# Latent attention: the value products of a head pair in two blocks in place of five

## The chip, the cores and the metric

The kernel runs on one core of a Trainium2 chip. The metric is the device time of one execution in microseconds; lower is better. Here TensorE is also called PE, VectorE DVE, ScalarE ACT, GpSimd POOL and SyncE SP, as in the profile.

## The reference

Two blocks of a model are computed one after the other on 512 tokens of 1024 channels: feed forward, gated linear attention with a convolution, cross attention and again feed forward; then latent attention, a convolved feed forward, a pooling mixer and a last convolved feed forward. All inputs are float32. The change lies in the latent attention, which sees 16 meta tokens and the 512 tokens, 528 rows. The reference fills these up to 640 and goes through them in tiles of 128 queries:

```python
for start in range(0, L, Q_BLOCK):
    end = start + Q_BLOCK
    qb = q[:, start:end]; kb = k[:, :end]; vb = v[:, :end]
    s = jnp.einsum('bqhd,bkhd->bhqk', qb, kb).astype(jnp.float32) * scale
    s = jnp.where(mask[None, None], s, -jnp.inf)
    p = jax.nn.softmax(s, axis=-1).astype(vb.dtype)
    outs.append(jnp.einsum('bhqk,bkhd->bqhd', p, vb))
o = jnp.concatenate(outs, axis=1).reshape(B, L, N_HEADS * V_HEAD_DIM)
return o @ w_o
```

There are 16 heads, with values of 64 columns each.

## The kernel before

Every engine has its own instruction stream, written out by hand, and waits on semaphores. A `Signal` numbers its events in the order in which one engine produces them (`declare`), so that `wait(engine, key)` is a wait for a count; `pe_mla_order` gives the order of TensorE's events and must agree with the order in which `pe_mla` issues.

The latent attention goes over **8 pairs of heads**. The queries lie in five tiles `j`; tile 0 has the 16 meta rows, tiles 1 to 4 have 128 rows each, and tile `j` sees `j + 1` tiles of keys. A pair takes its tiles in the order `ITEMS = (4, 2, 1, 3, 0)`, each for both heads, which makes **10 turns** a pair and 80 in all (`SEQ`, counter `x`). "Turn 3 of pair 2" is `x = 23`.

What is done for a head and a tile:

- **Scores** (`pe_scores`, L3191): TensorE multiplies queries by keys into PSUM, for tiles 4, 2, 1 as one group and for tiles 3, 0 as the other. The scores of the heads ahead are made at turns 4, 6, 7 and 9 (`SCORES_AT`). A group waits until ScalarE has read the group of the head before it, whose place it takes.
- **Maxima** (L3430, VectorE), **probabilities** (`probs`, L3293, ScalarE: exponent and sum), then the division by the sum (L3440, L3441, VectorE).
- **Turn** (`pe_turn`, L3218): TensorE transposes the probabilities, `j + 1` pieces of 128 x 128, into PSUM pair 2. A tile of four or five pieces and a tile of head one share banks, so a turn waits for ScalarE's copy of the last one or of the one before.
- **Turned copy** (`turned_copy`, L3302): ScalarE copies the turned probabilities to `pt[:, x % 4]`, a ring of four slots with five rows of 128 each; tile `j` uses rows 0 to `j`. It waits for the value products that read the slot before.
- **Value products** (`pe_values`, L3242), one block for a tile and both heads: `j + 1` pieces times 2 heads, values (64 columns) as weights, the copies as moving data. Tile 4 goes to bank 1 of PSUM pair 3, tiles 2, 1, 3, 0 to bank 0. Each f32 product stands as two records in the trace.
- **Halves out** (`upper`, L3308, ScalarE; `lower`, L3446, VectorE): the output, split into `XHI` and `XLO`. Bank 1 is read at turn 5; bank 0 at turn 2 of the next pair. Tile 4's products wait for the read of bank 1 of the pair before, tile 2's for that of bank 0 (`("ol", p - 1, 0)`).

Beside the turns stand **jobs** (`pe_job`, L3171 and L3163): parts of the projections to queries, keys and values of later heads. In even pairs each of the ten turns has a job (`JOB_SLOTS`), in odd pairs turns 0, 1, 4, 6 and 8. Query and value jobs, and half of the key jobs, write bank 1 of PSUM pair 1, so such a job waits until VectorE has read the last one (L3565 for queries). Pair 6 has jobs at turns 0 to 3 alone, pair 7 none; in pair 0, turns 2 and 3 have none.

The place of a value block is set in `pe_mla`: block `y` of the whole sequence stands at turn `x = 2 y + 2`, behind the turn, the scores and the job of it, so at turns 2, 4, 6, 8 of its pair and turn 0 of the next:

```python
for x in range(len(SEQ)):
    pe_turn(pe, x)
    if scores_at(x):
        pe_scores(pe, n, *scores_at(x))
    for job in JOB_AT[x]:
        pe_job(pe, n, job)
    if x % 2 == 0 and x:
        pe_values(pe, n, x // 2 - 1)
```

From turn 1 of pair 7 on, parts of the output projection (L854, L856, L858) go in between, and behind the loop the rest of it.

Of the kernel before, what the change touches and what calls it, by code (L numbers as in the profile page):

```python
# [21 lines left out]
P = 128  # L22
# [3 lines left out]
META = 16  # L26
# [18 lines left out]
MH, NOPE, ROPE, VD = 16, 64, 32, 64  # L45
# [120 lines left out]
def program(nc, ctx, A, out):  # L166
# [2673 lines left out]
    NI = len(ITEMS)  # L2840
# [64 lines left out]
    def scores_at(x):  # L2905
# [5 lines left out]
        return (h, g) if h < MH else None  # L2911

    def pe_mla_order():
        o = [("s", h, g) for h in range(2) for g in range(2)]
        for x in range(len(SEQ)):
            o.append(("t", x))
            if scores_at(x):
                o.append(("s",) + scores_at(x))
            if x % 2 == 0 and x:
                o.append(("pv", x // 2 - 1))  # L2920
        return o + [("pv", len(SEQ) // 2 - 1)]

# [74 lines left out]
    def pe_mla(pe):  # L2997
# [54 lines left out]
# [3 lines that stand above are left out]
                pe_scores(pe, n, *scores_at(x))  # L3055
            for job in JOB_AT[x]:
                pe_job(pe, n, job)
            if x % 2 == 0 and x:
                pe_values(pe, n, x // 2 - 1)
            if x in EARLY_OUT:  # L3060
                pe_mla_out(pe, n + 3 * MH // 4, *EARLY_OUT[x])
        pe_values(pe, n, len(SEQ) // 2 - 1)
        n += 3 * MH // 4
# [157 lines left out]
    def pe_values(pe, n, y):  # L3221
# [14 lines left out]
        act_m.wait(pe, ("tc", 2 * y + 1))  # L3236
        nq = META if j == 0 else P
        for i in range(j + 1):
            for a in range(2):
                h, p0 = 2 * p + a, VD * a  # L3240
                dst = PS[3][p0:p0 + VD, 1, 0:P] if j == 4 else PS[3][p0:p0 + VD, 0, QROW[j]:QROW[j] + nq]
                ins = nc.tensor.matmul(dst, v4[:, h // 4 % 2, i, h % 4 * VD:(h % 4 + 1) * VD], pt[:, (2 * y + a) % 4, i, 0:nq],  # L3242
                                       start=(i == 0), stop=(i == j))
# [20 lines left out]
    def act_mla(act):  # L3264
# [31 lines left out]
        def turned_copy(x):  # L3296
            h, j = SEQ[x]
            pe_m.wait(act, ("t", x))
            if x >= 4:
                pe_m.wait(act, ("pv", x // 2 - 2))  # L3300
            nq = P if j else META
            act_m.inc(nc.scalar.activation(pt[:, x % 4, 0:j + 1, 0:nq], turn_at(x).rearrange("p (i q) -> p i q", q=P)[:, :, 0:nq],  # L3302
                                           ACT.Copy), ("tc", x))
# [1001 lines left out]
```

How the kernel before makes its waits and increments, by code:

```python
    def wait(self, eng, key):  # L124
        eng.wait_ge(self.sem, self.order[key])
# [463 lines left out]
    def slot_free(act, n):  # L589
        if n == MIX_HELD:
            dve_mix.wait(act, ("c", 3))
        elif n == XAT_HELD:
            pe_x.wait(act, ("s", 7))
        elif N_DOWN <= n < N_DOWN + 5:
            act.wait_ge(unit_summed, PHASE["cffn0"] + 4)
        elif N_DOWN + 5 <= n < N_DOWN + 7:
            act.wait_ge(hid_lo, 3 * FT)
        elif N_DOWN + 7 <= n < N_POOL + 4:
            act.wait_ge(unit_summed, N_DOWN)
        elif N_CF1 <= n < N_CF1 + 4:
            act.wait_ge(unit_summed, N_DOWN + 5)
        elif N_CF1 + 4 <= n < N_CF1 + 6:
            act.wait_ge(unit_summed, N_POOL + 4)
        elif n in (LAST + 2, LAST + 3):
            act.wait_ge(unit_summed, LAST)
        elif n >= LAST + 4:
            act.wait_ge(unit_summed, n - 3)
        elif O_OUT + 2 <= n < O_OUT + 5:
            act.wait_ge(unit_summed, O_OUT)
        elif O_OUT + 5 <= n < O_OUT + KD:
            pe_m.wait(act, ("s", MH - 1, 1))
        elif PHASE["cffn0"] <= n < PHASE["cffn0"] + 4:
            pe_m.wait(act, ("pv", len(SEQ) // 2 - 1))
        else:
            act.wait_ge(unit_summed, n - (PHASE["cffn0"] + 4) + O_OUT + 1)
# [31 lines left out]
    def sp_unit(sp, n, it, u):  # L648
# [1 line left out]
        if z and n >= z.n + RAW:  # L650
            v = (n - z.n) // 2 - 2
            sp.wait_ge(st_lo_dve, z.lo_dves + 4 * v + 4)
            if n % 2 == z.n % 2:
                sp.wait_ge(st_lo_pool, z.lo_pools + 3 * v + 2)
            else:
```

## Time and profile before

| | us |
|---|---|
| median of 3 runs | 2193.51 |
| lowest, highest | 2193.27, 2195.99 |
| profiled execution, own time | 2193.65 |
| its span | 2191.9 |
| loop of turns, first turn to last value block | 1170.9 to 1331.4 |
| pairs 2 and 3 together | 1211.29 to 1253.95 |

The profile is of one execution. A timeline row has the start from the span's start and the duration, both in us, the engine, the line of the kernel, the operation, what it writes and reads, its shape and how many records it holds; in brackets stands the idle time ahead of it with what ended it. A matmul's record is about 0.28 us long while the next one may start 0.12 us behind it, so the distance of two starts is what a matmul takes of TensorE's time. The bracket counts idle time from the end of the record before, and is less than what the start is late by.

### The profile page before, as it was taken

What the parts mean: (1) busy time and instruction counts of PE and PEld (TensorE: products, weight loads), DVE (VectorE), ACT (ScalarE), POOL (GpSimd) and SP (SyncE); (2) the same over time, 40 slices, a digit from 0 to 9 for tenths busy, and PEclk for the clock granted to TensorE, in tenths of its full rate; (3) what the DMA queues carried; (4) which work ended last, traced back from release to release, by engine and by line L of the source; (5) the groups of instructions that cost most, each with busy time, mean ns of one, the idle gap of its engine ahead of it and who ended that gap; (6) DMA issues with size and microseconds to landing.
All of it is one profiled execution on the core that took longest, in us unless ns stands there. A gap on an engine that the chain in (4) does not pass through costs nothing.

```text
span 2191.9 us, 37679 instructions
## 1 busy us (share of the span) xinstructions
PE 2163.7 (99%) x14613; PEld 1966.3 (90%) x14613; DVE 1353.5 (62%) x2137; ACT 1004.1 (46%) x1966; POOL 954.3 (44%) x724
## 2 busy tenths in 40 slices
PE   9999999999999999999999999999999999999998
PEld 7899998888888788989998889999999979999897
DVE  6794766637645557839568765762634698536266
ACT  5464553432443435636455556442433565424244
POOL 3644535642482456344452115244444504544443
PEclk9999999999999999999999999999999999999999
DMA  5333333331352223333321113133333303233331
GB/s 171 96 107 104 104 102 95 96 85 45 96 164 68 78 81 112 97 100 112 97 72 33 36 40 107 39 86 97 94 90 89 114 10 101 96 99 94 96 94 70
DMA packets 336811, 195.39 MB, mean 89 GB/s; under 512 B 7469, under 2 KB 327682, under 8 KB 336658
## 3 DMA queue, kind: packets, MB, share of 16 engines
q1 hardware_dynamic: 335570, 191.26, 29.8%
q8 instruction: 101, 1.65, 0.3%
q0 software_dynamic: 432, 0.79, 0.2%
q10 hardware_dynamic: 656, 1.25, 0.2%
q14 instruction: 52, 0.43, 0.1%
HBM read 190.39 MB, written 2.10 MB: 88 GB/s over the span
## 4 chain that ended last, share of the span: by engine, by line
PE 85%; DVE 8%; ACT 3%; issue 2%; POOL 1%; DVEq 0%; DMA 0%; ACTq 0%; SPq 0%; POOLq 0%
PE PS L854 17%; PE PS L858 17%; PE PS L856 17%; PE PS L1288 5%; PE PS L1290 5%; PE PS L1289 5%; PE PS L3191 2%; PE PS L3171 2%; PE PS L1209 2%; PE PS L1211 2%; PE PS L1210 2%; PE PS L3218 1%; PE PS L3242 1%; DVE u_conv L1745 1%; PE PS L2170 1%
## 5 line engine op out<-in xcount | busy, mean ns | idle before, releaser
L774 POOL TENSOR_TENSOR w_lo<-raw,w_hi 128x512 fp32r<-128x512 f32 (+5 forms) x559 | 740.9, 1348 | 920.6 <-ACT w_hi L790 919.0
L790 ACT ACTIVATE w_hi<-raw 128x512 fp32r<-128x512 f32 (+5 forms) x545 | 302.3, 603 | 454.2 <-PE PS L858 351.7
L854 PE MATMUL PS<-XHI,w_hi 128*128 128x264 f32 (+2 forms) x1720 | 412.4, 306 | 0.4 <-POOL w_lo L774 0.3
L858 PE MATMUL PS<-XHI,w_lo 128*128 128x264 f32 (+2 forms) x1720 | 406.2, 302 | 0.0
L856 PE MATMUL PS<-XLO,w_hi 128*128 128x264 f32 (+2 forms) x1720 | 405.7, 302 | 0.0
L854 PEld LDWEIGHTS PS<-XHI,w_hi 128*128 128x128 f32 x1720 | 276.3, 189 | 16.1 <-issue 2.4
L858 PEld LDWEIGHTS PS<-XHI,w_lo 128*128 128x128 f32 x1720 | 276.0, 189 | 12.6
L856 PEld LDWEIGHTS PS<-XLO,w_hi 128*128 128x128 f32 x1720 | 276.0, 189 | 12.1 <-issue 0.7
L854 PE MATMUL PS<-h_hi,w_hi 128*128 128x512 f32 (+2 forms) x588 | 179.7, 341 | 0.7 <-DVE h_lo L1771 0.7
L856 PE MATMUL PS<-h_lo,w_hi 128*128 128x512 f32 (+2 forms) x588 | 179.4, 341 | 0.0
L858 PE MATMUL PS<-h_hi,w_lo 128*128 128x512 f32 (+2 forms) x588 | 179.4, 341 | 0.0
L854 PEld LDWEIGHTS PS<-h_hi,w_hi 128*128 128x128 f32 x588 | 101.6, 188 | 13.8 <-issue 1.3
L858 PEld LDWEIGHTS PS<-h_hi,w_lo 128*128 128x128 f32 x588 | 101.6, 188 | 12.6
L856 PEld LDWEIGHTS PS<-h_lo,w_hi 128*128 128x128 f32 x588 | 101.6, 188 | 12.3
L755 POOL TENSOR_TENSOR w_lo<-raw,w_hi 128x512 fp32r<-128x512 f32 x48 | 67.5, 1409 | 94.9 <-ACT w_hi L1371 94.9
L755 POOL TENSOR_TENSOR sf_lo<-raw,sf_hi 128x512 fp32r<-128x512 f32 x48 | 68.3, 1426 | 78.8 <-ACT sf_hi L1371 78.8
L1533 ACT ACTIVATE h_hi<-hid 128x528 fp32r<-128x528 f32 (+4 forms) x56 | 35.7, 638 | 145.2 <-DVE hid L1769 145.1
L1745 DVE SCALAR_TENSOR_TENSOR u_conv<-u_buf,cols,u_conv 128x528 f32<-128x528 f32 (+1 forms) x44 | 62.3, 1415 | 50.5 <-ACT u_conv L1492 50.5
L1807 DVE SCALAR_TENSOR_TENSOR X<-PS,X 128x512 f32<-128x512 f32 x48 | 33.1, 689 | 86.7 <-PE PS L858 86.7
L1745 DVE SCALAR_TENSOR_TENSOR g_conv<-g_buf,cols,g_conv 128x528 f32<-128x528 f32 (+1 forms) x44 | 54.3, 1235 | 39.1 <-ACT g_conv L1511 39.1
L1771 DVE TENSOR_TENSOR h_lo<-hid,h_hi 128x512 fp32r<-128x512 f32 (+4 forms) x56 | 44.4, 794 | 43.4 <-ACT h_hi L1533 43.4
L1517 ACT ACTIVATE g_act<-g_conv 128x528 f32<-128x528 f32 (+1 forms) x44 | 28.1, 639 | 88.7 <-DVE g_conv L1748 88.7
(621 smaller groups left out, 5472.4 us busy)
## 6 DMA issues: line engine op xcount, KB each, us to landing
raw<-in_ffn_w_up SPq DMA_DIRECT2D x132, 512.0 KB, 3.7
raw<-in_ffn_w_down SPq DMA_DIRECT2D x70, 512.0 KB, 3.8
raw<-in_ffn_w_gate SPq DMA_DIRECT2D x44, 512.0 KB, 3.8
raw<-in_w_in SPq DMA_DIRECT2D x25, 512.0 KB, 3.6
raw<-in_ffn_w_down SPq DMA_DIRECT2D x24, 384.0 KB, 3.4
raw<-in_xattn_w_kv SPq DMA_DIRECT2D x16, 512.0 KB, 3.8
raw<-in_w_out SPq DMA_DIRECT2D x8, 512.0 KB, 4.0
raw<-in_xattn_w_q SPq DMA_DIRECT2D x8, 512.0 KB, 4.6
```

What stands on the lines that cost most here:

```text
L755: ins = nc.gpsimd.tensor_tensor(s_lo, seven_source(z, v, i), s_hi.bitcast(F32), ALU.subtract)
L774: ins = nc.gpsimd.tensor_tensor(d[:, c], r[:, c], h[:, c].bitcast(F32), ALU.subtract)
L790: ins = nc.scalar.activation(d, r, ACT.Copy)
L854: nc.tensor.matmul(ps, wh, ahi(k)[:, c:c + w], start=(k == 0), stop=False)
L856: nc.tensor.matmul(ps, wh, alo(k)[:, c:c + w], start=False, stop=False)
L858: ins = nc.tensor.matmul(ps, wl, ahi(k)[:, c:c + w], start=False, stop=(k == u.kt - 1))
L1209: nc.tensor.matmul(ps, h_hi[:, k, ts], s_hi[:, cs], start=start, stop=False)
L1288: nc.tensor.matmul(bank_, wh, xh, start=(k == 0 and i in (0, 1, 3)), stop=False, skip_group_check=True)
L1289: nc.tensor.matmul(bank_, wh, xl, start=False, stop=False, skip_group_check=True)
L1290: ins = nc.tensor.matmul(bank_, wl, xh, start=False, stop=(k == 3), skip_group_check=True)
L1745: nc.vector.scalar_tensor_tensor(cv_[:, 0:w], buf[:, 1:1 + w], tap(inv - 2, 1, ft), cv_[:, 0:w], ALU.mult, ALU.add).then_inc(conv_mid, 1)
L1771: nc.vector.tensor_tensor(h_lo[:, a + 2 * it, hidden_cols(blk)], hid[:, 0:w], h_hi[:, a + 2 * it, hidden_cols(blk)].bitcast(F32), ALU.subt ...
```

## The change

The value blocks of a pair stand at two turns: the products of tiles 4 and 2 behind the job of turn 3, those of tiles 1, 3 and 0 behind the job of turn 9. Pair 7 keeps its places. `values_at` gives them, for `pe_mla_order` and for `pe_mla`. The turned copy of tile 0 (turns 8 and 9) goes to row 4 of its slot, which only tile 4 uses besides, and no longer waits for the products that read rows 0 to 2 of the slot; the products of tile 0 read row 4. Everything below the new lines stands 7 lines lower in the file.

```diff
--- before.py
+++ after.py
@@ -2910,15 +2910,23 @@
         h = 2 * (x // (2 * NI)) + d
         return (h, g) if h < MH else None
 
+    VALUES_BEHIND = {3: (0, 1), 9: (2, 3, 4)}
+
+    def values_at(x):
+
+        p, at = x // (2 * NI), x % (2 * NI)
+        if p == PAIRS - 1:
+            return ([at // 2 - 1 + NI * p] if at and at % 2 == 0 else []) + ([NI * PAIRS - 1] if at == 2 * NI - 1 else [])
+        return [NI * p + y for y in VALUES_BEHIND.get(at, ())]
+
     def pe_mla_order():
         o = [("s", h, g) for h in range(2) for g in range(2)]
         for x in range(len(SEQ)):
             o.append(("t", x))
             if scores_at(x):
                 o.append(("s",) + scores_at(x))
-            if x % 2 == 0 and x:
-                o.append(("pv", x // 2 - 1))
-        return o + [("pv", len(SEQ) // 2 - 1)]
+            o += [("pv", y) for y in values_at(x)]
+        return o
 
 
     PROBS_AT = {0: ((1, 1),), 1: ((1, 3),), 2: ((1, 0),), 5: ((2, 4),), 6: ((2, 2), (2, 1)), 7: ((2, 3),),
@@ -3055,11 +3063,10 @@
                 pe_scores(pe, n, *scores_at(x))
             for job in JOB_AT[x]:
                 pe_job(pe, n, job)
-            if x % 2 == 0 and x:
-                pe_values(pe, n, x // 2 - 1)
+            for y in values_at(x):
+                pe_values(pe, n, y)
             if x in EARLY_OUT:
                 pe_mla_out(pe, n + 3 * MH // 4, *EARLY_OUT[x])
-        pe_values(pe, n, len(SEQ) // 2 - 1)
         n += 3 * MH // 4
         act_m.wait(pe, ("p", MH - 1, GROUPS[1][-1]))
         pe_out_half(pe, n, 1, 0, ks=range(KD - 1))
@@ -3234,12 +3241,12 @@
         if j == 4 and p % 2 == 0:
             pe.wait_ge(unit_read, n + kv_jobs(p // 2)[0].unit + 1)
         act_m.wait(pe, ("tc", 2 * y + 1))
-        nq = META if j == 0 else P
+        nq, i0 = (META, 4) if j == 0 else (P, 0)
         for i in range(j + 1):
             for a in range(2):
                 h, p0 = 2 * p + a, VD * a
                 dst = PS[3][p0:p0 + VD, 1, 0:P] if j == 4 else PS[3][p0:p0 + VD, 0, QROW[j]:QROW[j] + nq]
-                ins = nc.tensor.matmul(dst, v4[:, h // 4 % 2, i, h % 4 * VD:(h % 4 + 1) * VD], pt[:, (2 * y + a) % 4, i, 0:nq],
+                ins = nc.tensor.matmul(dst, v4[:, h // 4 % 2, i, h % 4 * VD:(h % 4 + 1) * VD], pt[:, (2 * y + a) % 4, i0 + i, 0:nq],
                                        start=(i == 0), stop=(i == j))
         pe_m.inc(ins, ("pv", y))
 
@@ -3296,10 +3303,10 @@
         def turned_copy(x):
             h, j = SEQ[x]
             pe_m.wait(act, ("t", x))
-            if x >= 4:
+            if x >= 4 and j:
                 pe_m.wait(act, ("pv", x // 2 - 2))
-            nq = P if j else META
-            act_m.inc(nc.scalar.activation(pt[:, x % 4, 0:j + 1, 0:nq], turn_at(x).rearrange("p (i q) -> p i q", q=P)[:, :, 0:nq],
+            nq, i0 = (P, 0) if j else (META, 4)
+            act_m.inc(nc.scalar.activation(pt[:, x % 4, i0:i0 + j + 1, 0:nq], turn_at(x).rearrange("p (i q) -> p i q", q=P)[:, :, 0:nq],
                                            ACT.Copy), ("tc", x))
 
         def upper(p, part):
```

TensorE in pair 2, from turn 2 to turn 5, before. `pt,v` are value products, `const,pr` transposes (the turns), `cq,w` a query job, `k,q` scores; the pieces left out are matmuls of the same job or the same scores:

```order
L3218 MATMUL PS<-const,pr 128x128 x3
...
L3171 MATMUL PS<-cq_hi,w_lo 128x264
L3242 MATMUL PS<-pt,v 64x128 x10
L3218 MATMUL PS<-const,pr 128x128 x3
...
L3171 MATMUL PS<-cq_hi,w_lo 128x264
L3218 MATMUL PS<-const,pr 128x128 x2
L3191 MATMUL PS<-k,q 128x512
...
L3171 MATMUL PS<-cq_hi,w_lo 128x264
L3242 MATMUL PS<-pt,v 64x128 x6
L3218 MATMUL PS<-const,pr 128x128 x2
```

And now:

```order
L3178 MATMUL PS<-cq_hi,w_lo 128x264
L3225 MATMUL PS<-const,pr 128x128 x3
L3178 MATMUL PS<-cq_hi,w_hi 128x264
...
L3178 MATMUL PS<-cq_hi,w_lo 128x264
L3249 MATMUL PS<-pt,v 64x128 x16
L3225 MATMUL PS<-const,pr 128x128 x2
L3198 MATMUL PS<-k,q 128x512
...
L3178 MATMUL PS<-cq_hi,w_lo 128x264
L3225 MATMUL PS<-const,pr 128x128 x2
L3178 MATMUL PS<-cq_hi,w_hi 128x264
```

The 10 products of tile 4 stood between the job of turn 2 and turn 3, and the 6 of tile 2 between the job of turn 4 and turn 5. All 16 now stand behind the job of turn 3; jobs 2 and 3, and jobs 4 and 5, have only transposes between them.

TensorE in pair 6, from turn 4 on, where there are no jobs, before:

```order
L3218 MATMUL PS<-const,pr 128x128 x2
L3191 MATMUL PS<-k,q 128x512
L3191 MATMUL PS<-k,q 128x16
L3191 MATMUL PS<-k,q 128x272
L3191 MATMUL PS<-k,q 128x144
L3242 MATMUL PS<-pt,v 64x128 x6
L3218 MATMUL PS<-const,pr 128x128 x6
L3191 MATMUL PS<-k,q 128x400
L3191 MATMUL PS<-k,q 128x16
L3242 MATMUL PS<-pt,v 64x128 x4
L3218 MATMUL PS<-const,pr 128x128 x4
L3191 MATMUL PS<-k,q 128x512
```

And now, from the block of turn 3 on:

```order
L3249 MATMUL PS<-pt,v 64x128 x16
L3225 MATMUL PS<-const,pr 128x128 x2
L3198 MATMUL PS<-k,q 128x512
L3198 MATMUL PS<-k,q 128x16
L3198 MATMUL PS<-k,q 128x272
L3198 MATMUL PS<-k,q 128x144
L3225 MATMUL PS<-const,pr 128x128 x6
L3198 MATMUL PS<-k,q 128x400
L3198 MATMUL PS<-k,q 128x16
L3225 MATMUL PS<-const,pr 128x128 x4
L3198 MATMUL PS<-k,q 128x512
```

Between the two large scores (`128x512`, of heads 14 and 15) stood the products of tiles 2 and 1. Now only transposes and the small scores stand there. On ScalarE and VectorE the instructions and their order are as before; the wait of the two copies of tile 0 in each pair is gone.

## Rows read from the trace of the kernel before

**Rows 1.** The page: the chain that ended last, shares of the span by engine.

```profile
PE 85%; DVE 8%; ACT 3%; issue 2%; POOL 1%; DVEq 0%; DMA 0%; ACTq 0%; SPq 0%; POOLq 0%
```

**Rows 2.** Busy us (x instructions) by stretch: PE, PEld, DVE, ACT, POOL, PEclk, DMA.

```profile
1211.29:1253.95 42.66, 42.30 (x356) 35.62 (x355) 30.04 (x109) 22.55 (x73) 7.73 (x13) 1.00 0.12 33
```

**Rows 3.** Timeline of TensorE, pair 2: start, us, line, out<-in, shape, records [idle before].

```profile
1214.90 0.29 PE L3171 MATMUL PS<-cq_hi,w_lo 128*128 128x264 f32 x1
1215.02 0.49 PE L3218 MATMUL PS<-const,pr 128*128 128x128 f32 x3
1215.71 0.39 PE L3171 MATMUL PS<-cq_hi,w_hi 128*128 128x264 f32 x1 [0.20 <-DVE q L3565]
...
1216.78 0.28 PE L3171 MATMUL PS<-cq_hi,w_lo 128*128 128x264 f32 x1
1216.99 1.31 PE L3242 MATMUL PS<-pt,v 128*64 128x128 f32 x20
1218.24 0.55 PE L3218 MATMUL PS<-const,pr 128*128 128x128 f32 x3
1218.54 0.37 PE L3171 MATMUL PS<-cq_hi,w_hi 128*128 128x264 f32 x1
...
1222.91 0.88 PE L3242 MATMUL PS<-pt,v 128*64 128x128 f32 x12
1223.72 0.44 PE L3218 MATMUL PS<-const,pr 128*128 128x128 f32 x2
...
1225.09 0.60 PE L3218 MATMUL PS<-const,pr 128*128 128x128 f32 x4
1225.52 0.96 PE L3191 MATMUL PS<-k,q 128*128 128x400 f32 x4
...
1228.19 0.66 PE L3218 MATMUL PS<-const,pr 128*128 128x128 f32 x4
1228.69 1.95 PE L3191 MATMUL PS<-k,q 128*128 128x512 f32 x8
```

**Rows 4.** Timeline of TensorE, start of pair 3.

```profile
1236.67 0.29 PE L3242 MATMUL PS<-pt,v 128*64 128x16 f32 x4
1236.91 0.75 PE L3218 MATMUL PS<-const,pr 128*128 128x128 f32 x5
...
1239.00 1.31 PE L3242 MATMUL PS<-pt,v 128*64 128x128 f32 x20
```

**Rows 5.** Timeline of VectorE, pair 2.

```profile
1215.22 0.43 DVE L3565 TENSOR_TENSOR q<-PS,ct 128x264 f32<-128x264 f32 x1 [1.05 <-PE PS L3171]
...
1216.72 0.57 DVE L3446 TENSOR_TENSOR XLO<-PS,XHI 128x400 fp32r<-128x400 f32 x1 [0.53 <-ACT XHI L3308]
1217.21 0.42 DVE L3565 TENSOR_TENSOR q<-PS,ct 128x264 f32<-128x264 f32 x1
...
1223.33 0.43 DVE L3565 TENSOR_TENSOR q<-PS,ct 128x264 f32<-128x264 f32 x1
```

**Rows 6.** Timeline of ScalarE, start of pair 3.

```profile
1236.06 0.71 ACT L3302 ACTIVATE pt<-PS 128x640 f32<-128x640 f32 x1 [1.52 <-PE PS L3218]
```

**Rows 7.** Timeline of VectorE, from turn 7 of pair 2 into pair 3.

```profile
1230.67 0.72 DVE L3430 CUSTOM_DVE_ANT_0 PS<-PS,causal 128x528 f32<-128x528 f32 x1 [1.93 <-PE PS L3191]
...
1240.87 0.57 DVE L3446 TENSOR_TENSOR XLO<-PS,XHI 128x400 fp32r<-128x400 f32 x1
```

**Rows 8.** Timeline of TensorE, pair 6 from turn 4 on.

```profile
1306.00 1.95 PE L3191 MATMUL PS<-k,q 128*128 128x512 f32 x8
...
1311.99 2.02 PE L3191 MATMUL PS<-k,q 128*128 128x512 f32 x8 [0.45 <-ACT pr L3293]
...
1315.24 0.97 PE L3191 MATMUL PS<-k,q 128*128 128x400 f32 x4
1316.53 0.74 PE L3218 MATMUL PS<-const,pr 128*128 128x128 f32 x5 [0.32 <-ACT pt L3302]
```

**Rows 9.** Timeline of ScalarE, pair 6, turn 8.

```profile
1314.40 0.20 ACT L3293 ACTIVATION_READ_ACCUMULATOR pr<-PS,mst 128x1 f32 x1
```

## The prediction

> **What bounds the kernel now.** I read the chain of work first: TensorE carries 85% of it [rows 1]. The change touches one stage, the loop of the latent attention over 80 turns, so next comes the table by stretch over two head pairs in its middle: TensorE is busy for 42.30 of 42.66 us, at the full granted clock, while VectorE has 30.04 us and ScalarE 22.55 us [rows 2]. So whatever TensorE no longer does there should shorten the stage, unless one of its waits takes the place. To see that, I go through the timeline of TensorE row by row and look at start to start, since a matmul's record overlaps the next one's. Each f32 product is two records there, so the product "x10" of the order is "x20" in the trace.
>
> **What a block of value products costs beyond its products.** Blocks of 20 and 12 records run from their first start to the next instruction's start for 1.25 and 0.81 us [rows 3]. That is 0.055 us a record and 0.15 us a block besides. Ahead of a block, the last matmul of the job is followed after 0.21 us (1216.78 to 1216.99), where a turn follows a job after 0.12 (1214.90 to 1215.02): 0.09 more. Behind it, four turns take 0.50 us up to the scores (1228.19 to 1228.69), and 0.43 behind a job (1225.09 to 1225.52): 0.06 more [rows 3]. So a block has 0.30 us that isn't products. The Trainium skill (TensorEngine Tiling, Key Properties) says that a change of tiling mode drains TensorE; the value products are the only ones with 64 columns, and the trace agrees with 0.30 us a block. By that rule alone this change could only gain.
>
> Seven of the eight pairs go from five blocks to two (the last pair is left as it was), which is 21 blocks fewer. Fourteen of them are full ones at 0.30. The seven of tile 0 take 0.24 us to the next turn for 4 records [rows 4], of which 0.15 to 0.22 stays when they stand inside a block; I take 0.20 saved with what lies around them. The **gain** is 14 x 0.30 + 7 x 0.20 = 5.6 us, if nothing else moves.
>
> **What the blocks covered.** A block was also the filler between two things of which the second waits for ScalarE or VectorE. The same matmuls run now, but two steps later or one step earlier. I list each place where a block leaves.
>
> (a) Jobs of the dense pairs. In pairs 2, 4 and 6 turns 0 to 3 have a job each, and all these jobs write PSUM bank 1 of PS1: a job starts only when VectorE has read the one ahead. That hand-over is in the trace: last matmul 1214.90, VectorE's read 1215.22 for 0.43, next job 1215.71 [rows 3, 5]. So 0.81 us must lie between, and only the step from the job (0.12) and three turns (0.30 behind values, 0.24 here) do: 0.44 us of waiting at turn 2, today as after. Turn 3 now has the same: the block of tile 4 that stood between job 2 and turn 3 goes behind job 3. Job 2's last matmul is at 1216.78, so job 3 could start at 1217.14, but the read of job 2 stands behind the XLO row of 1216.72 and is at 1217.21 for 0.42 [rows 5]: job 3 waits until 1217.69, 0.55 us. At turn 1 the cover was tile 0's block; the step of 0.12 and five turns (0.24 + 2 x 0.11) lie between, so 0.2 us of wait appears. In pair 6 that job waits already, so this counts twice. 3 x 0.55 + 2 x 0.2 = **2.0 us**.
>
> (b) Turn 5 of pairs 0, 2 and 4. The block of tile 2 left the place between job 4 and turn 5. VectorE first does the three maxima of the new scores, then reads job 4, at 1223.33 for 0.43 [rows 5]; job 5 can't start before 1223.82. Today TensorE reaches it at 1223.91, 1223.72 and two turns (0.30 - 0.11) [rows 3]. The block's leaving moves TensorE up to 1222.95 (1222.91 was the block's start, less 0.09 for the step into it, plus two turns without the 0.06, 0.13), and there it waits 0.87 us. 3 x 0.87 = **2.6 us**. So in this place nearly nothing of the 1.1 us block is won, while its products are paid at turn 3.
>
> (c) Turn 1 of pairs 1, 3 and 5. It waits for ScalarE's copy of turn 0 (1236.06 for 0.71, turn at 1236.91) [rows 4, 6]. Tile 0's block in between, 0.24 + 0.09, comes out and the turn stays where it was: 0.33 of wait. The next even pair gives 0.1 back at its turn 0, which trailed ScalarE. 3 x 0.33 - 3 x 0.1 = **0.7 us**.
>
> (d) Tile 2's products of pairs 1, 3 and 5 now come at turn 3, not at 4, and need the lower half of the pair before, read by VectorE (it and tile 1, 3, 0 share bank 0 of PS3). VectorE has no idle time from the maxima at 1230.67 to that read, which ends at 1240.87 + 0.57 = 1241.44 [rows 7]. TensorE's way from the scores' start at 1228.69 to tile 4's products is 10.31 us today (1239.00) [rows 3, 4]; the new one has tile 1's 8 records more (0.44), two block overheads less (0.50), the wait of (c) (0.33), turn 3 (0.33) and tile 4's products (1.15) before tile 2's: 12.1 us. VectorE is there after 12.8. 0.7 us is the end above; I take 0.5, since VectorE's rows may be shorter once shifted: 3 x 0.5 = **1.5 us**.
>
> (e) Pair 6 has no jobs behind turn 3. Its scores of head 15 start 5.99 us behind those of head 14 (1306.00, 1311.99), and wait for ScalarE, 0.5 us start to start [rows 8]. Two blocks stand in between now, 1.7 us with their overhead; they leave, the distance stays, and the wait grows by 1.7. The second scores of head 15 wait for probabilities that ScalarE has at 1314.60 [rows 9]: about 0.6 more. The block at turn 9 then fills the 0.5 us ahead of the turn at 1316.53 (1.29 us behind the scores where 0.81 do) [rows 8], which is given back, and the next turn is again as in (c), 0.3. Together 1.7 + 0.6 - 0.5 + 0.3 = **2.1 us**.
>
> Each new wait also costs some 0.02 us of restart, 0.3 in all. ScalarE's copies of tile 0, which no longer wait for a value block, bring nothing of their own: nobody was late for them. Without the free row the change couldn't be made, since they would wait for products that stand behind them. ScalarE and VectorE keep their order and work.
>
> **The sum**: 2.0 + 2.6 + 0.7 + 1.5 + 2.1 + 0.3 = 9.2 lost, 5.6 won, **3.6 us slower**; I take 3.4, since (a), (b) and (d) are read at one pair each and VectorE's rows differ a little between pairs. Behind the loop TensorE runs matmul on matmul to the end, so it passes through. The profiled execution took 2193.65 us (span 2191.9), 0.14 above the median of 2193.51. 2193.5 + 3.4 = 2196.9.
>
> **Rivals.**
> - *The drains win.* Faster. If the hand-overs turn out covered (the job's read on VectorE comes sooner when TensorE's work is moved, as the read hangs on the job's end alone in (a) and on the maxima in (b)), the 5.6 us come through, less what waits anyway: 2188.5. Against it: the wait of 0.44 at turn 2 is there in the rows, without a block between. It decides where less than a fifth of the 9.2 us shows up. 8%. The rule of the Trainium skill on draining (TensorEngine Tiling) stands behind this case.
> - *Half and half.* The waits of (b) and (d) are read from one place; if VectorE is 0.3 to 0.5 us sooner there, and the tail's chain tightens, some 3 us of the loss go: 2191 to 2195. 20%.
> - *The drain is paid per tile.* The 0.15 us may belong to a group that changes its accumulator and waits on a semaphore, not to the change of mode. Then the merged block keeps it: 21 x 0.15 = 3.2 us less won, 2200. For it: no two groups of value products stand together today, so no row excludes it. Against: two turns of different heads in a row cost nothing extra. 17%.
> - *Not what it says*: the order shows two blocks a pair, so no.
>
> **How the numbers follow.** The forecast has 55%, with its own range 2195 to 2199. What a measurement of this kernel can tell from no change is about 0.2%, 4.4 us: 2189.1 to 2197.9. Faster: the first rival, 8%. Slower: a quarter to a third of the forecast and the third rival, 30%. The rest, 62%, is the same. The range leaves out the first rival and the end of the third: 2191.5 to 2200.0.
>
> **What would show it.** In the profile after: values in blocks of 32 and 28 records, with one 0.2 us gap to each side (right), a gap of 0.2 inside them (third rival). Waits of TensorE for "DVE q" at turns 1, 2, 3 and 5 of pairs 2 and 4, 0.4 to 0.9 us start to start; for XLO ahead of tile 2's products in odd pairs; 2.2 us ahead of head 15's scores. Two pairs in the middle take 43.3 to 43.6 us against 42.66. If they take under 42.2, (a) to (d) are wrong; if the loop's loss sits elsewhere, the sum is.

## The result and the profile after

The changed kernel takes **2198.79 us** in the median of 19 executions (2197.07 to 2202.58), the kernel before 2194.39 in the same number (2192.27 to 2200.47). The ratio is 1.002, with a 95% interval of 1.0014 to 1.0026: 3.1 to 5.7 us slower. The prediction said 2196.9, 3.4 us slower.

The profiled execution took 2201.40 us (span 2199.6), 2.6 above its median, so I don't compare the spans but the loop, from the start of the first turn to the start of the last value products. Its length is in the table by stretch (columns as in [rows 2]: length, then busy us of TensorE, its weight loads, VectorE, ScalarE, GpSimd; granted clock; DMA share; GB/s). The kernel before:

```profile
1170.88:1331.19 160.31, 156.31 (x1326) 130.67 (x1324) 111.00 (x393) 90.85 (x280) 35.03 (x44) 1.00 0.13 36
```

The changed kernel:

```profile
1175.75:1339.38 163.63, 153.41 (x1325) 131.20 (x1323) 110.35 (x393) 90.83 (x280) 35.05 (x43) 1.00 0.13 36
```

The loop is **3.32 us** longer, at the full granted clock in both. TensorE is recorded busy for 2.90 us less and idle for 6.22 us more (10.22 against 4.00). That is the prediction's outline, less work and more waiting. (The two differences are not exactly gain and loss, since a matmul's record reaches over the next one's start; the steps below count from start to start.) The loop also starts 4.87 us later in this execution. That is ahead of the change: the table shows two stretches of it below the full clock, which the kernel before has at 1.00.

```profile
500.00:560.00 60.00, 60.00 (x327) 48.90 (x326) 43.99 (x70) 15.77 (x27) 12.36 (x8) 0.97 0.20 62
1140.00:1165.00 25.00, 23.52 (x170) 22.54 (x169) 21.20 (x34) 14.84 (x28) 9.72 (x11) 0.93 0.16 45
```

A second profile of the same kernel has the loop's start at 1172.44 and its length at 163.54 us, so the start is a matter of the execution and the length is not. (One other profile has the same two stretches at a lower clock, that of second_only below, 0.97 and 0.93.)

What TensorE waits for in the loop (waiting line, what for, us in total, times, longest), first the kernel before:

```profile
PE PS L3218 <- DVE pr L3441: 1.3, 2, 0.7
PE PS L3171 <- DVE q L3565: 1.0, 4, 0.4
PE PS L3218 <- ACT pt L3302: 1.0, 5, 0.3
...
```

and the changed one (its line numbers are those of before plus 7):

```profile
PE PS L3178 <- DVE q L3572: 3.8, 10, 0.6
PE PS L3198 <- ACT pr L3300: 2.6, 2, 2.1
PE PS L3225 <- ACT pt L3309: 1.8, 7, 0.9
PE PS L3249 <- DVE XLO L3453: 0.9, 3, 0.4
...
```

Jobs waiting for VectorE's read of the job ahead go from 1.0 to 3.8 us, and a wait for the lower half (XLO) is new. In the chain of work, VectorE's part falls from 8% [rows 1] to 7% and TensorE's rises from 85 to 87% (a second profile of this kernel has VectorE at 8%), which doesn't tell the waits apart; the timeline does.

Timeline of TensorE in pair 2, the answer to [rows 3] (start, us, line, out<-in, shape, records, idle before):

```profile
1218.05 0.28 PE L3178 MATMUL PS<-cq_hi,w_lo 128*128 128x264 f32 x1
...
1218.86 0.39 PE L3178 MATMUL PS<-cq_hi,w_hi 128*128 128x264 f32 x1
...
1221.81 0.28 PE L3178 MATMUL PS<-cq_hi,w_lo 128*128 128x264 f32 x1
1221.93 0.49 PE L3225 MATMUL PS<-const,pr 128*128 128x128 f32 x3
1222.73 0.39 PE L3178 MATMUL PS<-cq_hi,w_hi 128*128 128x264 f32 x1 [0.31 <-DVE q L3572]
...
1223.81 0.28 PE L3178 MATMUL PS<-cq_hi,w_lo 128*128 128x264 f32 x1
1224.02 1.97 PE L3249 MATMUL PS<-pt,v 128*64 128x128 f32 x32
1225.92 0.44 PE L3225 MATMUL PS<-const,pr 128*128 128x128 f32 x2
...
1229.07 0.38 PE L3225 MATMUL PS<-const,pr 128*128 128x128 f32 x2
1230.07 0.39 PE L3178 MATMUL PS<-cq_hi,w_hi 128*128 128x264 f32 x1 [0.62 <-DVE q L3572]
```

(Where steps are counted, "three turns" means, as in the prediction, three transposes, the pieces of one turn.) Job 3 starts 0.92 us behind job 2's last matmul (1221.81 to 1222.73), where the step of 0.12 and three turns (0.24) would take 0.36: it waits 0.56. Job 1 waits 0.23 (1218.05 to 1218.86, less 0.12 and 0.46 for five turns), although the view puts no wait beside its row. Job 5 follows its two turns after 1.00 us instead of 0.13: 0.87. The merged block runs 1.90 us for 32 records, from 1224.02 to 1225.92.

Pair 3, the answer to [rows 4]:

```profile
1243.04 0.74 PE L3225 MATMUL PS<-const,pr 128*128 128x128 f32 x5 [0.16 <-ACT pt L3309]
...
1245.44 1.31 PE L3249 MATMUL PS<-pt,v 128*64 128x128 f32 x20
1247.02 0.88 PE L3249 MATMUL PS<-pt,v 128*64 128x128 f32 x12 [0.27 <-DVE XLO L3453]
```

Tile 2's products come 1.58 us behind the start of tile 4's; 20 records without a wait take 1.14 to the next record's start, so 0.44 is waited for XLO. Pair 6, the answer to [rows 8]:

```profile
1313.44 1.95 PE L3198 MATMUL PS<-k,q 128*128 128x512 f32 x8
...
1319.43 2.02 PE L3198 MATMUL PS<-k,q 128*128 128x512 f32 x8 [2.10 <-ACT pr L3300]
1321.29 0.38 PE L3225 MATMUL PS<-const,pr 128*128 128x128 f32 x2
1322.19 1.04 PE L3198 MATMUL PS<-k,q 128*128 128x400 f32 x4 [0.51 <-ACT pr L3300]
1323.15 1.60 PE L3249 MATMUL PS<-pt,v 128*64 128x128 f32 x28
1324.69 0.76 PE L3225 MATMUL PS<-const,pr 128*128 128x128 f32 x5
1326.34 0.74 PE L3225 MATMUL PS<-const,pr 128*128 128x128 f32 x5 [0.89 <-ACT pt L3309]
```

The large scores of heads 14 and 15 are 5.99 us apart, to the hundredth what they were [rows 8]. What stood between them has become idle time.

### The profile page after: what moved, and what is told of

It is laid out like the page before. It is cut to its first block, busy times and chain, and to the rows that moved or that the text cites. A ratio compares the mean times of both kernels' runs of the same rounds, so it can differ in the third digit from the quotient of the medians.

```text
span 2199.6 us, 37663 instructions
## 1 busy us (share of the span) xinstructions
PE 2166.1 (98%) x14613; PEld 1971.8 (90%) x14613; DVE 1352.7 (61%) x2137; ACT 1004.5 (46%) x1966; POOL 955.7 (43%) x724
## 3 DMA queue, kind: packets, MB, share of 16 engines
q8 instruction: 101, 1.65, 0.3%
## 4 chain that ended last, share of the span: by engine, by line
PE 87%; DVE 7%; ACT 3%; issue 2%; POOL 0%; DMA 0%; DVEq 0%; ACTq 0%; SPq 0%; POOLq 0%
PE PS L854 18%; PE PS L858 18%; PE PS L856 18%; PE PS L1288 5%; PE PS L1290 5%; PE PS L1289 5%; PE PS L1209 2%; PE PS L1210 2%; PE PS L1211 2%; PE PS L3198 2%; PE PS L3178 2%; PE PS L3225 1%; PE PS L3249 1%; PE PS L2050 1%; PE PS L2170 1%
## 5 line engine op out<-in xcount | busy, mean ns | idle before, releaser
L3309 ACT ACTIVATE pt<-PS 128x640 f32<-128x640 f32 (+4 forms) x80 | 37.8, 473 | 68.5 <-PE PS L3225 67.8
```

## The experiments

Two theories were put against each other.

- **Theory W (waits)**: a value block taken out saves its 0.30 us, and where it stood between two things of which the second waits for VectorE or ScalarE, the wait it covered comes out. The loop's length is the sum of such places.
- **Theory L (lateness)**: the products come later than before, so everything behind them (the halves out, the buffers of turned probabilities) is late, and VectorE and ScalarE with it. Then it matters how late the products are, and not between what they stand.

A third was the rival of the prediction by which the 0.15 us is paid for each tile's group.

All kernels but two have a table in place of the rule of the change: for each pair and each of the tiles 4, 2, 1, 3, 0, the turn at which its products are issued, and 0 for ahead of that turn's job or 1 for behind it. A turn of 10 or 11 is turn 0 or 1 of the next pair. Tile 0's free row is kept in all of them. The edit to the changed kernel:

```diff
-    VALUES_BEHIND = {3: (0, 1), 9: (2, 3, 4)}
+    PLACES = (
...
-            o += [("pv", y) for y in values_at(x)]
+            o += [("pv", y) for side in range(2) for y in values_at(x, side)]
...
+            for y in values_at(x, 0):
+                pe_values(pe, n, y)
             for job in JOB_AT[x]:
                 pe_job(pe, n, job)
-            for y in values_at(x):
+            for y in values_at(x, 1):
                 pe_values(pe, n, y)
```

In the table's words the change is ((3,1),(3,1),(9,1),(9,1),(9,1)) for pairs 0 to 6, the kernel before ((2,1),(4,1),(6,1),(8,1),(10,1)). Pair 7 stays as it was in all but placed.

What all of them gave (loop against the 160.31 us of before; blocks of value products in the loop; the median's ratio, or "one" where only one time was taken; the kernel before ran beside each at 2193.69 to 2194.47):

| kernel | blocks | loop, us | against before | expected | time, us | ratio (95%) |
|---|---|---|---|---|---|---|
| before | 40 | 160.31 | | | 2194.39 | |
| after | 19 | 163.63 | +3.32 | +3.4 | 2198.79 | 1.002 (1.0014 to 1.0026) |
| second_only | 26 | 158.91 | -1.40 | -0.9 | 2194.19 | 0.9995 (0.9985 to 1.0005) |
| first_only | 33 | 166.48 | +6.17 | +4.4 | 2199.64 | 1.0018 (1.0009 to 1.0028) |
| ahead_of_job | 19 | 163.69 | +3.38 | +1.9 | 2197.15 | 1.0009 (1.0 to 1.0019) |
| pair6_back | 22 | 161.68 | +1.37 | +1.6 | 2195.11 | one |
| after_again | 19 | 163.54 | +3.23 | +3.3, or +4.9 at a lower clock | 2198.03 | one |
| odd_only | 31 | 160.64 | +0.33 | -0.6 | 2194.13 | one |
| turn5_ahead | 19 | 162.51 | +2.20 | 1.2 below after | 2196.28 | one |
| block_cut | 48 | 162.89 | +2.58 | +2.4 | 2196.82 | 1.0012 (1.0002 to 1.0022) |
| placed | 30 | 156.94 | -3.37 | -3.7 | 2190.71 | 0.9985 (0.9976 to 0.9994) |
| second_pair6 | 28 | 158.11 | -2.20 | -1.9 to -2.1 | 2191.66 | 0.999 (0.9981 to 0.9999) |

And by pair (from a pair's first turn to the next pair's, us), which shows where each difference sits:

| kernel | 0 | 1 | 2 | 3 | 4 | 5 | 6 | pair 7 |
|---|---|---|---|---|---|---|---|---|
| before | 21.78 | 18.63 | 24.03 | 18.63 | 24.03 | 18.76 | 19.80 | 14.65 |
| after | 22.10 | 18.62 | 24.91 | 18.54 | 24.75 | 18.54 | 21.47 | 14.69 |
| second_only | 21.53 | 18.35 | 23.76 | 18.35 | 23.63 | 18.34 | 20.26 | 14.69 |
| first_only | 22.38 | 19.43 | 25.17 | 19.08 | 25.18 | 19.56 | 21.02 | 14.65 |
| ahead_of_job | 22.10 | 18.54 | 24.38 | 18.53 | 24.23 | 18.63 | 22.59 | 14.69 |
| turn5_ahead | 22.21 | 18.67 | 24.41 | 18.66 | 24.27 | 18.65 | 20.96 | 14.69 |
| odd_only | 21.78 | 19.09 | 23.88 | 18.74 | 23.88 | 19.09 | 19.53 | 14.66 |
| block_cut | 22.08 | 18.93 | 24.34 | 18.94 | 24.35 | 19.06 | 20.16 | 15.03 |
| placed | 20.38 | 19.29 | 22.59 | 19.29 | 22.46 | 19.29 | 19.60 | 14.04 |

The number of blocks alone doesn't order the kernels: 19 blocks give 162.51 to 163.69 us, 30 give 156.94, 31 give 160.64, 33 give 166.48. Two things in the table by pair are bookkeeping: tile 0's products count to the pair in which they stand, and placed puts tiles 3 and 0 of an even pair into the odd one behind it. So its odd pairs are longer, while pairs 2 and 3 together take 41.88 us against 42.66 before.

### The two halves of the change alone

**second_only** merges tiles 1, 3 and 0 at turn 9 and leaves tiles 4 and 2 where they were, in pairs 0 to 6:

```diff
-        ((3, 1), (3, 1), (9, 1), (9, 1), (9, 1)),
+        ((2, 1), (4, 1), (9, 1), (9, 1), (9, 1)),
```

> The blocks of tiles 4 and 2 are back at turns 2 and 4; only tiles 1, 3 and 0 are one block at turn 9. The loop is measured from the first turn to the last value block: 160.3 us before, 163.6 in the changed kernel. Theory W (each block taken out saves about 0.3 us, and lays bare a wait of a job or turn wherever it was the cover): 14 blocks fewer save 3.5 to 3.9 us; the waits at turns 3 and 5 of the dense pairs and for XLO ahead of tile 2 are gone, those at turn 1 (0.2 and 0.3) and the tail of pair 6 stay in part: loop 0.9 us shorter than before, time 0.3 to 1.5 us less. Theory L (what costs is that the value products come late, for the copies, the ring and the halves out): these three tiles are as late as in the changed kernel, the other two are on time: between before and the change, 1 to 2 us slower than before.

The loop is 1.40 us **shorter** than before. Where tile 4 stands behind job 2, job 3 no longer waits. TensorE there:

```profile
1218.85 0.28 PE L3187 MATMUL PS<-cq_hi,w_lo 128*128 128x264 f32 x1
1219.06 1.31 PE L3258 MATMUL PS<-pt,v 128*64 128x128 f32 x20
...
1220.61 0.37 PE L3187 MATMUL PS<-cq_hi,w_hi 128*128 128x264 f32 x1
```

Its products of tiles 1 and 3 come as late as those of after, tile 1's three turns later than in the kernel before. By theory L this had to lengthen the loop. Only the loop shows it: the median is 0.28 us below that of before, and the interval of the ratio reaches over 1.

**first_only** does the other half, tiles 4 and 2 at turn 3:

```diff
-        ((3, 1), (3, 1), (9, 1), (9, 1), (9, 1)),
+        ((3, 1), (3, 1), (6, 1), (8, 1), (10, 1)),
```

> Tiles 4 and 2 in one block at turn 3, tiles 1, 3 and 0 at turns 6, 8 and 0 of the next pair as before. Theory W: only 7 blocks fewer (2.1 us), but the waits of (a) at turn 3, (b) at turn 5 and (d), and head 15's scores: 2.0 to 6.5 us lost, loop 4.4 us longer than before, so slower than the changed kernel with fewer changes. Theory L: two of five tiles late: less than the change, 1 to 2 us slower than before.

The loop is 6.17 us longer, so the loss is all in this half, as theory W had it; but that is 1.8 us more than I expected of W, and further still from L. The rows tell where. What TensorE waits for there:

```profile
PE PS L3258 <- DVE XLO L3462: 2.2, 3, 0.9
```

The wait for XLO is 2.2 us recorded against 0.9 in the changed kernel (the jobs wait 3.8 us in both). In pair 1 of first_only:

```profile
1197.47 1.31 PE L3258 MATMUL PS<-pt,v 128*64 128x128 f32 x20
1199.65 0.88 PE L3258 MATMUL PS<-pt,v 128*64 128x128 f32 x12 [0.86 <-DVE XLO L3462]
```

That is 2.18 us less 1.14, a wait of 1.04; pair 5 has the same, pair 3 has 0.68, 2.8 us in all. After has 0.53, 0.44 and 0.44 in pairs 1, 3 and 5, 1.4 us. The difference, 1.3 us, is most of the miss. VectorE there comes to XLO without a pause, behind the last of the reads of keys:

```profile
1197.46 0.87 DVE L3587 TENSOR_TENSOR k<-PS,r_kv 64x264 f32<-64x264 f32 x2
...
1198.56 0.43 DVE L3457 TENSOR_SCALAR pr<-pr,mst 128x400 f32<-128x400 f32 x1
1199.02 0.57 DVE L3462 TENSOR_TENSOR XLO<-PS,XHI 128x400 fp32r<-128x400 f32 x1
```

Pair 3 has the same reads. But VectorE pauses there for 0.30 us ahead of the one at 1238.27, having taken 0.23 us at 1236.70 for an instruction of 16 columns that took 0.87 in pair 1 (1192.09). So VectorE reaches XLO about 0.35 us sooner after the scores in pair 3, which is the difference of the two waits. Why that instruction took longer in pair 1 is open.

The wait is a difference of two arrivals. In pair 3, counted from the start of turn 7's scores, VectorE lets tile 2's products start after 12.46 us in first_only and after 12.88 in after, and TensorE would be there after 11.78 and 12.44. TensorE is 0.66 us earlier and VectorE only 0.42. In the changed kernel TensorE has tile 1's eight records (0.44) and the wait of (c) (0.33) on that way, and one block less (0.30); in first_only it has neither of the two. That makes 0.47 of the 0.66. The two halves don't add up for this reason: -1.40 and +6.17 make +4.77, and the whole is +3.32.

**odd_only** makes the change in pairs 1, 3 and 5 alone; pairs 0, 2, 4 and 6 each have the row of the kernel before:

```diff
-        ((3, 1), (3, 1), (9, 1), (9, 1), (9, 1)),
+        ((2, 1), (4, 1), (6, 1), (8, 1), (10, 1)),
```

> Only pairs 1, 3 and 5 have the two blocks of the change; all others have their five as before. Theory W (waits laid bare, terms (c) and (d) only): the odd pairs take 18.5 us against 18.6 to 18.8, the even ones 0.1 less through the start: loop 0.6 us shorter than before. Theory L (lateness costs): odd pairs longer by half a microsecond each.

A miss by 0.9 us. The odd pairs take 0.46, 0.11 and 0.33 us more than before, so this run taken alone looks more like theory L, which had half a microsecond for each. The rows show it to be the same miss as in first_only: tiles 4 and 2 stand at turn 3 of an odd pair, and the even pair ahead of it has not moved tile 1's products onto TensorE's way. TensorE's three waits for XLO add up to 2.2 us here too, the longest 0.9, which is 1.3 us more than in after. So the step (d) of the prediction is worth 1.4 us only together with what the change does in the even pairs. Alone it costs about twice that (2.8 us start to start). This explanation was found after both misses; no run tested it with a forecast of its own.

### Where the products stand, with the number of blocks kept

**ahead_of_job** puts tiles 4 and 2 at the same turn 3, ahead of its job:

```diff
-        ((3, 1), (3, 1), (9, 1), (9, 1), (9, 1)),
+        ((3, 0), (3, 0), (9, 1), (9, 1), (9, 1)),
```

> The changed kernel with one thing moved: the block of tiles 4 and 2 stands at turn 3 ahead of the job instead of behind it. Theory W: it covers the hand-over between jobs 2 and 3 (0.55 us in each of pairs 2, 4 and 6), all other waits stay: loop 1.6 us shorter than in the changed kernel, 1.9 longer than before. Theory L: no difference beyond 0.3 us against the changed kernel, since the products come at the same turn.

Pairs 2 and 4 take 24.38 and 24.23 us, 0.53 and 0.52 less than in after: job 3's wait of 0.55 is covered by the block. The products are the same ones in the same turn. Theory L has no place for that difference, theory W names it. The loop as a whole came out at +3.38 and not +1.9, which by itself would fit theory L (no difference to after). The pairs show why it doesn't: pair 6 takes 22.59 us, 1.12 more than in after. Timeline of TensorE there:

```profile
1309.15 1.95 PE L3207 MATMUL PS<-k,q 128*128 128x512 f32 x8
...
1315.14 3.65 PE L3207 MATMUL PS<-k,q 128*128 128x512 f32 x8 [2.10 <-ACT pr L3309]
1318.62 0.38 PE L3234 MATMUL PS<-const,pr 128*128 128x128 f32 x2
```

The same eight records that take 2.02 us in after take 3.65. The granted clock of the stretch:

```profile
1315.10:1318.60 3.50, 3.46 (x8) 2.22 (x9) 1.11 (x7) 1.07 (x3) 0.00 (x0) 0.52 0.28 84
```

It is 0.52, the lower of the two levels (1.2 GHz), right behind the wait of 2.10 us; in after, behind the same wait, it is 1.00 (1319.43 to 1321.45). Without these 1.63 us the loop would be at +1.75, near the +1.9 expected.

**after_again** is the changed kernel once more, to see whether the clock falls there too.

> The changed kernel once more, for a second profile. In the run ahead_of_job the scores of head 15 behind the 2.1 us wait ran at a granted clock of 0.52 and took 1.6 us longer; in the first profile of the changed kernel, behind a wait of the same length, they didn't. If the clock falls there by chance of the moment, this profile may show either: the loop is 163.6 us, or 165.2 with the scores at 3.65 us in place of 2.0. Everything else in the loop repeats within 0.2 us.

The pairs agree with the first profile within 0.1 us, and the scores take 2.02 us behind a wait of 2.10:

```profile
1316.04 2.02 PE L3198 MATMUL PS<-k,q 128*128 128x512 f32 x8 [2.10 <-ACT pr L3300]
```

So the clock fell in one of three profiles with this wait of 2.10 us. What TensorE did ahead of it doesn't tell them apart: it was busy for 3.05 of the 5.00 us from 1310 to 1315 in ahead_of_job, which ends with the wait, and for 3.03 of the 5.10 us from 1314.3 to 1319.4 in after.

**turn5_ahead** puts tiles 4 and 2 ahead of job 5, two turns later than the change:

```diff
-        ((3, 1), (3, 1), (9, 1), (9, 1), (9, 1)),
+        ((5, 0), (5, 0), (9, 1), (9, 1), (9, 1)),
```

> The changed kernel with the block of tiles 4 and 2 at turn 5, ahead of its job, in place of turn 3. Theory W: it covers the hand-over between jobs 4 and 5 (0.87 us in pairs 0, 2, 4), while job 3 still waits 0.55, and job 6 may wait 0.3: pairs 2 and 4 take about 0.5 us less than in the changed kernel (24.9, 24.75), pair 6 0.5 less if the clock holds, loop 1.2 us shorter than the changed one. Theory L: the products come two turns later than in the changed kernel, so the loop grows.

The loop is 1.12 us shorter than in after, with later products and the same 19 blocks. Theory L has the wrong sign here too.

**pair6_back** gives pair 6 its five blocks back and keeps the rest:

```diff
-        ((3, 1), (3, 1), (9, 1), (9, 1), (9, 1)),
+        ((2, 1), (4, 1), (6, 1), (8, 1), (10, 1)),
```

> The changed kernel with the five blocks of pair 6 at their old places. Theory W with term (e): pair 6 falls from 21.5 to about 19.7 us (19.8 before), the wait ahead of head 15's scores from 2.2 to 0.5 us; loop 1.6 us longer than before, 1.9 less than the change. If the loss were spread over the pairs evenly, the loop would fall by 0.5 us only.

Pair 6 goes from 21.47 to 19.55 us and the others stay within 0.1: of the 3.32 us 1.95 come back, 1.92 of them in this pair. The wait ahead of head 15's scores is 0.45 us recorded again, as in [rows 8].

### What a block costs by itself

**block_cut** is the kernel before with one value block of each pair cut in two (tile 4's, shown against the changed kernel, whose rule it takes back: the first two pieces behind turn 2's job, the other three behind turn 3's transposes, ahead of its job). The change to 64 columns and back comes eight times more, and no product moves past a job or scores.

```diff
+            if x % (2 * NI) == 3:
+                pe_values(pe, n, x // 2 - 1, range(2, 5))
...
-            for y in values_at(x):
-                pe_values(pe, n, y)
+            if x % (2 * NI) == 2:
+                pe_values(pe, n, x // 2 - 1, range(2))
+            elif x % 2 == 0 and x:
+                pe_values(pe, n, x // 2 - 1)
```

> The kernel before with one block more in each pair: tile 4's products are cut in two, the transposes of turn 3 between them. Nothing else moves. If each entry into the value products and back costs about 0.3 us of TensorE, the loop grows by 0.3 in each of the 8 pairs, 2.4 us (2.0 to 2.6, less where TensorE waits anyway). If the cost belonged to the start of a group of products (its first product into an empty accumulator, its wait), nothing is added, since the second part goes on in the same accumulator: 0 to 0.4 us.

The loop is 2.58 us longer, 0.32 a block, and each pair between 0.30 and 0.38. The rows of pair 2:

```profile
1219.97 0.66 PE L3248 MATMUL PS<-pt,v 128*64 128x128 f32 x8
1220.56 0.55 PE L3224 MATMUL PS<-const,pr 128*128 128x128 f32 x3
1221.04 0.88 PE L3248 MATMUL PS<-pt,v 128*64 128x128 f32 x12
1221.85 0.39 PE L3177 MATMUL PS<-cq_hi,w_hi 128*128 128x264 f32 x1
```

The waits for VectorE's read are those of the kernel before:

```profile
PE PS L3177 <- DVE q L3572: 1.0, 4, 0.4
```

So this is the price of a block alone. Here one accumulation is cut within a tile: the second part goes on in the same accumulator and asks for the same semaphores, long met, and the cut costs the full price. In the changed kernel the block of tiles 4 and 2 takes 1.90 us for 32 records, which is 0.055 a record and 0.15 once. That of tiles 1, 3 and 0 takes 1.54 for 28: 0.055 for each of 24 records, 0.15 once, and 0.07 for tile 0's four, which have 16 columns. With 0.15 for each tile they would take 2.05 and 1.84. The price hangs on leaving the value products and coming back, not on the tile: the rival is out.

### Blocks taken out only where nothing behind them waits

If theory W holds, a block should be merged where it covers nothing, and be put where a wait is. **second_pair6** is second_only with pair 6 left as before:

```diff
         ((2, 1), (4, 1), (9, 1), (9, 1), (9, 1)),
-        ((2, 1), (4, 1), (9, 1), (9, 1), (9, 1)),
+        ((2, 1), (4, 1), (6, 1), (8, 1), (10, 1)),
         ((2, 1), (4, 1), (6, 1), (8, 1), (9, 1)),
```

> As second_only (tiles 1, 3 and 0 in one block at turn 9, the others as before), with pair 6 as in the kernel before. The loop of second_only was 1.4 us shorter than before while its pair 6 was 0.5 longer, with waits of 1.2 and 0.5 us ahead of head 15's scores. Theory W: pair 6 back at 19.6 to 19.8, loop 1.9 to 2.1 us shorter than before, time 0.1% less, at the edge of what five rounds can tell.

**placed** chooses for each place. In pairs 0, 2 and 4, tile 4 covers job 3's wait, tiles 2 and 1 together that of job 5, and tiles 3 and 0 follow at the next pair's first turn. In pairs 1, 3 and 5 tiles 1 and 3 are together, tile 2 is left until its XLO is there, and tile 0 goes behind job 1 of the next pair, where it covers job 2's wait of 0.44, which the kernel before has too:

```diff
+        ((2, 1), (5, 0), (5, 0), (10, 0), (10, 0)),
+        ((2, 1), (6, 0), (8, 1), (8, 1), (11, 1)),
...
+        ((2, 1), (5, 0), (6, 1), (8, 1), (10, 1)),
+        ((4, 0), (6, 1), (8, 1), (9, 0), (9, 1)),
```

> Blocks are taken out only where no job or turn waits behind them, by the hand-overs read in the traces so far. Pairs 0, 2, 4: tile 4 at turn 2, tile 2 with tile 1 ahead of the job of turn 5, tiles 3 and 0 ahead of the job of turn 0 of the next pair. Pairs 1, 3, 5: tile 4 at turn 2, tile 2 ahead of the job of turn 6, tiles 1 and 3 at turn 8, tile 0 at turn 1 of the next pair. Pair 6 as before but for tile 2 ahead of the job of turn 5, pair 7 spread by half turns. Theory W: two blocks fewer in each of pairs 0, 2 and 4, one in each odd pair, 9 in all, 2.7 us, and the present waits at turn 2 and turn 12 shortened or covered: loop 3.7 us shorter than before, 156.6 us; time 2190 against 2194, ratio 0.998. Theory L: tile 3 and tile 0 later, so no gain.

Both are shorter than before: the loops by 2.20 and 3.37 us, the times by ratios of 0.999 (0.9981 to 0.9999) and 0.9985 (0.9976 to 0.9994). placed is the fastest of all kernels here, with 30 blocks. (The expectation counted nine fewer than before; it is ten, since nothing stands between the last two blocks of pair 7.) In its pair 2:

```profile
1213.27 0.28 PE L3187 MATMUL PS<-cq_hi,w_lo 128*128 128x264 f32 x1
1213.48 0.29 PE L3258 MATMUL PS<-pt,v 128*64 128x16 f32 x4
...
1214.08 0.39 PE L3187 MATMUL PS<-cq_hi,w_hi 128*128 128x264 f32 x1
...
1221.19 0.38 PE L3234 MATMUL PS<-const,pr 128*128 128x128 f32 x2
1221.51 1.31 PE L3258 MATMUL PS<-pt,v 128*64 128x128 f32 x20
1222.75 0.39 PE L3187 MATMUL PS<-cq_hi,w_hi 128*128 128x264 f32 x1
```

Job 2 starts 0.81 us behind job 1's last matmul, which is the hand-over, as in the kernel before; but tile 0's products now stand within it, so they cost nothing. Job 5 starts right behind its 20 records. Of the waits for VectorE's read one is left, 0.6 us.

## Why the prediction came out

**The bound** was read rightly: the loop moved by what TensorE waits, and nothing behind it made up for that.

**The gain, 0.30 us a block.** Holds: 0.32 by block_cut, and 1.90 and 1.54 us for the merged blocks. The Trainium skill (TensorEngine Tiling, Key Properties) has the drain at a change of mode, and the runs agree with it: 0.32 us for going to 64 columns and back once more, nothing for the change of tile within a block. It decides the time only where nothing waits: in second_pair6 the rule gives a gain, in first_only seven blocks fewer go with 6.17 us more.

**(a) Job 3 and job 1.** 0.56 and 0.23 in pair 2, forecast 0.55 and 0.2. Job 3's is confirmed by an edit, the 0.53 and 0.52 us of ahead_of_job.

**(b) Job 5.** 0.87, forecast 0.87. Confirmed by turn5_ahead and by placed, in which 20 records stand in that place and pair 2 is 1.44 us shorter than before.

**(c) Turn 1 of odd pairs.** From the last matmul ahead of it, 1242.59, to 1243.04 are 0.45 us, where the step takes 0.12: 0.33, as forecast. Pairs 1 and 5 have the same.

**(d) XLO.** 0.53, 0.44 and 0.44, forecast 0.5 each. Both arrival times were a little off in the same direction. From the scores of turn 7 (1234.14) to tile 2's products (1247.02) are 12.88 us; I had VectorE there after 12.8. TensorE would have been there after 12.44, where I had 12.1. The size was right for this kernel, but I took it along to first_only and odd_only as if it were a property of the place. There it is 0.68 to 1.04, since TensorE arrives earlier. That is the one step of my working that the experiments corrected, and it isn't a step of the forecast's sum but of its use. It was near by some luck: the wait is a difference of two arrivals 12 us behind the scores, and it grew by 0.2 to 0.6 us when the other half of the change was left out.

**(e) Pair 6.** The scores 5.99 us apart, the wait 2.10 recorded where it was 0.45 (forecast: 1.7 more); the second scores wait 0.68 start to start (1321.29 to 1322.19, less 0.22 for two transposes), forecast 0.6; the 0.5 given back and the 0.3 behind it are there too (1324.69 follows the block at once; 1326.34 follows after 1.65, where the kernel before takes 1.62 with tile 0's block in between). With job 3's wait and the three blocks saved, the terms make 2.65 - 0.8 = +1.85 for the pair; it measures +1.67.

**The sum.** 3.6 worked out, 3.4 taken, 3.32 and 3.23 in two profiles of the loop. Pairs 2 and 3 take 43.45 us, in the forecast 43.3 to 43.6. Read start to start at every place of the loop, the new waits come to (a) 2.1, (b) 2.6, (c) 0.6, (d) 1.4 and (e) 2.2 us, 8.9 in all, which is what the five terms of the prediction add up to. That leaves 5.6 us for the gain less the restarts, forecast 5.3 (5.6 less 0.3). So the sum did not come out by errors that cancel. The nearness is still better than the steps deserve: two pairs' rows stood for seven, and pairs alike differ by up to 0.2 us.

**The medians** differ by 4.4 us, 1.1 more than the loops. (Of the 1.9 us by which the median lies above the forecast time, 0.9 is the kernel before, which took 2194.39 beside it and 2193.51 in the prediction.) The interval, 3.1 to 5.7, holds 3.3, so it may be spread. But the mean granted clock of each of the 19 executions of the changed kernel is on record. Nine have 0.999, and their median is 2197.68, 3.3 above the median of before (whose 19 clocks are not); ten have 0.998 or 0.997, with times from 2197.96 to 2202.58. Of the 58 executions of the kernel before that ran beside the experiments, ten have 0.998 or less. They ran at other times than the changed kernel, so the comparison is a loose one. By it the changed kernel seems to lose the full clock more often, and the extra 1.1 us goes with those executions. Where the clock falls in them is not shown. Pair 6's wait is one candidate, at 1.63 us in the one profile of ahead_of_job; neither of the two profiles of this kernel has it, and the one at 0.997 lost its time ahead of the loop, where the change does nothing. It stays open.

**The rivals.** "The drains win" fell with the waits at each place where it needed none. "Half and half" (2191 to 2195) would have had the loop below +1.5. "The drain is paid per tile" fell with block_cut and with the merged blocks' lengths.

## What to carry to other kernels

A small group of instructions between two others is worth its own time plus the wait that it covers: look up, for each place from which it leaves, what the next instruction waits for, and when that is ready. Here a hand-over from TensorE over VectorE and back takes 0.81 us when VectorE is free, from the start of the last matmul to the start of the next, and longer when it is not (0.92 to job 3, 1.12 to job 5); whatever stands between is free up to that length, so the list of places is short and can be read from start times. Merge groups only where nothing behind them waits, and spend the ones that remain on the waits that are there: 30 blocks in chosen places beat both 40 spread evenly and 19 merged. When the effect of an edit is a difference of two arrival times, measure both ends again before you use it in another version.

## What was not expected of the hardware

- **The granted clock fell without a long pause of TensorE.** In ahead_of_job it fell behind a single wait of 2.10 us, to 0.52 (the 1.2 GHz level), for the eight records behind it, which took 3.65 us instead of 2.02. In two other profiles with the same wait it stayed at 1.00. It isn't this wait alone: in the first profile of the changed kernel and in that of second_only the clock fell twice ahead of the loop. In the changed kernel's, the second of these begins near 1154.1, 2.2 us behind the end of a wait of 1.48 us, with TensorE recorded busy for 3.62 of the 5.10 us ahead; the kernel before has the same wait (1.47 us, busy 3.53 of 5.00) and goes on at 1.00. The first, near 526.1, has no wait ahead of it at all: TensorE is recorded busy for 6.00 of the 6.00 us from 520 to 526. So a single profile may or may not show a fall, and the one inside the loop cost 1.63 us; what decides it, the runs here don't show.
- **A block of 64-column products has one long gap near its start**, 0.154 us between its second and third record, where all later ones alternate between 0.006 and 0.103. In the merged block of 32 records there is no second such gap at the change from tile 4 to tile 2, though the accumulator, the PSUM bank and the semaphore awaited change there. A change of those three cost nothing that can be read. Nor does the gap stand for the change to 64 columns: in pair 3, where tile 2's products wait for XLO behind tile 4's, it is there again between their second and third record, with no other kind of matmul in between. A pause is enough for it.
